# A hybrid mLSTM and GLA layer: alpha by stacked halves, the last norm with features on partitions, and three reorderings

## The reference

```
h = rmsnorm(x, g1) * (1 + scale1) + shift1 ;  z = h @ w_in
la = log_sigmoid(lr_b @ w_alpha + b_alpha) / 16      # rank 16, 4 heads of 128: the forget gates of GLA
x  = x + gate1 * ((sig(g_a) * mlstm(...) + sig(g_b) * gla(q_b, k_b, v_b, la)) @ w_out)
h2 = rmsnorm(x, g2) * (1 + scale2) + shift2
x  = x + gate2 * ((silu(h2 @ w_gate) * (h2 @ w_up)) @ w_down)
y  = rmsnorm(x, g_final)                             # the last norm
```

## Time and profile before

| what | us |
| --- | --- |
| median of 3 runs | 1948.06 (1946.88 to 1949.89) |
| the profiled execution, whole | 1946.07 |
| its span, first to last instruction | 1944.3 |
| TensorE busy in the span | 1897.1 |
| VectorE, ScalarE, GpSimd busy | 1062.3, 681.8, 681.9 |

### The profile page before, as it was taken

One profiled execution on the slowest core, in us unless ns is written; L12 is line 12 of the kernel. 1 busy time (PEld: TensorE's weight loads), 2 busy tenths in 40 slices (PEclk: granted clock), 3 DMA queues, 4 the chain that ended last, 5 costly groups with the idle time before them and its releaser, 6 DMA issues. The chain is left out here.

```text
span 1944.3 us, 33250 instructions
## 1 busy us (share of the span) xinstructions
PE 1897.1 (98%) x13205; PEld 1813.6 (93%) x13205; DVE 1062.3 (55%) x1900; ACT 681.8 (35%) x1425; POOL 681.9 (35%) x582
## 2 busy tenths in 40 slices
PE   7899999999999999999999999999999999999997
PEld 4899999999999989999898999999999999999996
DVE  5740554414553226534164578786756666566657
ACT  4523423334234243342343554322232223322333
POOL 3221322212232213313132485334454345444541
PEclk8999999999999999999999999999999999999999
DMA  9241222332222322224133553102121112111212
GB/s 335 72 100 50 74 77 55 105 84 69 71 62 73 104 79 71 55 62 128 54 85 105 176 157 99 44 23 66 44 66 42 47 45 66 50 39 44 66 44 101
DMA packets 211266, 155.07 MB, mean 80 GB/s; under 512 B 10196, under 2 KB 195732, under 8 KB 210600
## 3 DMA queue, kind: packets, MB, share of 16 engines
q1 hardware_dynamic: 210810, 152.73, 26.6%
q10 hardware_dynamic: 302, 0.22, 0.0%
HBM read 131.42 MB, written 21.50 MB: 79 GB/s over the span
## 5 line engine op out<-in xcount | busy, mean ns | idle before, releaser
L1264 POOL TENSOR_TENSOR w_lo<-w_raw,w_hi 128x512 fp32r<-128x512 f32 x128 | 180.5, 1410 | 714.6 <-ACT w_hi L1087 714.6
L919 PE MATMUL bank<-h_hi,w_hi 128*128 128x352 f32 x1536 | 328.7, 336 | 1.3 <-ACT w_hi L1087 1.3
L919 PE MATMUL bank<-h_hi,w_lo 128*128 128x352 f32 x1536 | 313.4, 326 | 1.2 <-POOL w_lo L1264 1.1
L919 PE MATMUL bank<-h_lo,w_hi 128*128 128x352 f32 x1536 | 312.9, 325 | 0.0
L919 PEld LDWEIGHTS bank<-h_hi,w_hi 128*128 128x128 f32 x1536 | 257.0, 190 | 16.5 <-issue 12.1
L919 PEld LDWEIGHTS bank<-h_hi,w_lo 128*128 128x128 f32 x1536 | 260.3, 190 | 2.7 <-POOL w_lo L1264 2.7
L919 PEld LDWEIGHTS bank<-h_lo,w_hi 128*128 128x128 f32 x1536 | 260.4, 190 | 0.0
L2287 POOL TENSOR_TENSOR f_lo<-w_raw,f_hi 128x512 fp32r<-128x512 f32 x107 | 143.0, 1341 | 201.8 <-ACT f_hi L2111 201.7
L2287 POOL TENSOR_TENSOR w_lo<-w_raw,w_hi 128x512 fp32r<-128x512 f32 x107 | 144.2, 1352 | 149.3 <-ACT w_hi L2111 149.2
L2625 DVE SCALAR_TENSOR_TENSOR x_t<-bank,ada,x_t 128x352 f32<-128x352 f32 (+1 forms) x288 | 156.1, 568 | 56.0 <-PE bank L2042 38.8
L1087 ACT ACTIVATE w_hi<-w_raw 128x512 fp32r<-128x512 f32 x128 | 80.1, 626 | 166.4 <-PE bank L919 166.4
(11 more groups left out here) (480 smaller groups left out, 3864.5 us busy)
## 6 DMA issues: line engine op xcount, KB each, us to landing
w_raw<-in_w_in SPq DMA_DIRECT2D x128, 256.0 KB, 3.0
w_ada_tile<-in_w_ada SPq DMA_DIRECT2D x32, 512.0 KB, 4.3
w_raw<-in_w_out SPq DMA_DIRECT2D x48, 256.0 KB, 2.9
w_raw<-in_w_ffn_gate SPq DMA_DIRECT2D x44, 256.0 KB, 3.0
w_raw<-in_w_ffn_up SPq DMA_DIRECT2D x44, 256.0 KB, 3.0
w_raw<-in_w_ffn_down SPq DMA_DIRECT2D x44, 256.0 KB, 2.7
w_ada_ring<-in_w_ada SPq DMA_DIRECT2D x8, 1024.0 KB, 7.8
x_scratch<-x_turned_rows SPq DMA_DIRECT2D x1, 4224.0 KB, 14.0
```

What stands on the lines that cost most here:

```text
L919: last = pe.matmul(g.ps[b][:, 0:n], x[:, s, k, :], y[:, 4 * h + k, c0:c0 + n], start=(h == 0 and k == 0 and m == 0), stop=(h == 1 and k == ...
L1264: pool.tensor_tensor(Wl[:, s], raw[:, r], Wh[:, s].bitcast(F32), ALU.subtract).then_inc(s_lo, 1)
```

## The change

- Alpha. Three groups of 16 rows are stacked at partitions 0, 32 and 64 of `xal` (high, low, high half of the inputs) and of `wal` (high, high, low half of the weights), in fp32r, with zeros between, so one product sums the three. Four heads times three matmuls of 352 columns replace the float32 ones. New stages `alpha_hi` and `alpha_lo` of head 0 make the halves on ScalarE and VectorE. `rows` and the loaded weights (three loads) live in a buffer of the values `v_b` until that is filled; the small loads and the first evacuation wait for x to be stored.
- `ada3` and `level0` of window A go from slot 39 to 40.
- In the first `out` step of the last third, ScalarE's square of the step before comes ahead of the two `h2_hi`.
- `last_third` replaces the last two pieces of the first plain unit: first weight half of gate and of up, then second half of each.
- In the first seven-product unit ScalarE makes weight halves 3 and 4 ahead of the product copies, and t copies 14 and 15 go between later halves; VectorE takes `form(15)` and the low halves 14 and 15 behind the first addition.
- The last norm with features on partitions. In the last down block ScalarE squares each piece of x and scales it in place by the gain, GpSimd adds the squares of features groups 1 to 6 into 352 columns a third, VectorE adds the last. TensorE multiplies these sums by a column of ones, which gives a mean square per token in a bank; root, reciprocal, and after the transposes VectorE scales the left and ScalarE the right half of each row tile. Six banks instead of eight serve the transposes. The gains, 8 numbers per partition, are loaded in the middle of `out`.

The diff, cut to its core:

```diff
-    "A": [("decay", 1), ("ada_load0", 2), ("scores", 6), ("keys", 6), ("interq", 8),
+    "A": [("decay", 1), ("ada_load0", 2), ("alpha_hi", 3), ("alpha_lo", 9), ("scores", 6), ("keys", 6), ("interq", 8),
...
-        rows = sb("gate_rows", [P, T])
+        setup_rows = V[1][:, :, :].rearrange("p n v -> p (n v)")
+        rows, w_rows = setup_rows[:, 0:T], setup_rows[:, T:T + QK]
+        xal = sb("alpha_inputs", [P, T], F32R)
...
-        wal = sb("w_alpha_all", [P, QK])
+        wal = sb("w_alpha_all", [P, QK], F32R)
...
-                     (m0[:, :], a["state_m"][0].rearrange("b h -> h b")), (wal[64:64 + RANK, :], a["w_alpha"][0])]
+                     (m0[:, :], a["state_m"][0].rearrange("b h -> h b"))]
+            small += [(w_rows[r:r + RANK, :], a["w_alpha"][0]) for r in (0, 32, 64)]
...
+            sp.wait_ge(g.s_xst, 16)
...
-                        for b, (c0, m) in enumerate(PARTS):
-                            full(pe.matmul(use(n + b)[:, 0:m], wal[64:64 + RANK, i * DK:(i + 1) * DK], rows[64:64 + RANK, c0:c0 + m], start=True, stop=True))
+                        pe.wait_ge(s_rows, 4)
+                        for c in range(NPC):
+                            c0, m = span(c)
+                            full(pe.matmul(use(n + c)[:, 0:m], wal[0:64 + RANK, i * DK:(i + 1) * DK], xal[0:64 + RANK, c0:c0 + m],
+                                           start=True, stop=True))
...
+                    elif name == "alpha_hi" and i == 0:
+                        act.wait_ge(s_r3, 1)
+                        for r in (0, 64):
+                            act.activation(xal[r:r + RANK, :], rows[64:64 + RANK, :], ACT.Copy)
+                        for r in (0, 32, 64):
+                            last = act.activation(wal[r:r + RANK, :], w_rows[r:r + RANK, :], ACT.Copy)
+                        last.then_inc(s_rows, 1)
+                    elif name == "alpha_lo" and i == 0:
+                        act.wait_ge(s_rows, 3)
+                        act.activation(xal[32:32 + RANK, :], rows[64:64 + RANK, :], ACT.Copy)
+                        act.activation(wal[64:64 + RANK, :], w_rows[64:64 + RANK, :], ACT.Copy).then_inc(s_rows, 1)
...
+                    elif name == "alpha_hi" and i == 0:
+                        dve.wait_ge(s_rows, 2)
+                        dve.tensor_tensor(rows[64:64 + RANK, :], rows[64:64 + RANK, :], xal[64:64 + RANK, :].bitcast(F32), ALU.subtract)
+                        dve.tensor_tensor(w_rows[64:64 + RANK, :], w_rows[64:64 + RANK, :], wal[64:64 + RANK, :].bitcast(F32),
+                                          ALU.subtract).then_inc(s_rows, 1)
...
+            def last_third(pl):
+
+                c0, n = span(NPC - 1)
+                pe.wait_ge(s_smh, 1)
+                for h in range(2):
+                    pe.wait_ge(s_hh, (NPC - 1) * KC + 4 * h + 4)
+                    for t in range(2):
+                        bnk, turns = pl.piece(3 * t + NPC - 1)
+                        if h == 0:
+                            wait(pe, s_pf[bnk], turns)
+                        s, _, before = pl.half(2 * t + h)
+                        pe.wait_ge(s_hi, before + 1)
+                        for m, (x, y) in enumerate(((Wh, g.Hh), (Wh, g.Hl), (Wl, g.Hh))):
+                            if m == 1 and t == 0:
+                                pe.wait_ge(s_sml, 1)
+                                pe.wait_ge(s_hl, (NPC - 1) * KC + 4 * h + 4)
+                            if m == 2:
+                                pe.wait_ge(s_lo, before + 1)
+                            for kk in range(4):
+                                last = pe.matmul(g.ps[bnk][:, 0:n], x(s)[:, kk, :], y[:, 4 * h + kk, c0:c0 + n],
+                                                 start=(h == 0 and kk == 0 and m == 0), stop=(h == 1 and kk == 3 and m == 2))
+                        if (h, t) != (0, 1):
+                            last.then_inc(s_used, 1 + h * t)
...
+            def mean_squares(c):
+
+                pe.wait_ge(s_fm, c + 1)
+                if c < 2:
+                    bnk, turns = lastp.piece(22 + c)
+                    pe.wait_ge(s_pf[bnk], turns + 1)
+                else:
+                    pe.wait_ge(s_rt, NPC + 1)
+                for t in DONE_WITH[c]:
+                    n = P if t < NC else NS
+                    last = pe.matmul(MS[c][0:n, t:t + 1], SQX[:, t * P:t * P + n], one, start=True, stop=True)
+                last.then_inc(s_sum, 1)
...
+            turn(0)
+            mean_squares(0)
+            turn(1)
+            mean_squares(1)
+            turn(2)
+            mean_squares(2)
+            for t in range(3, NT):
+                turn(t)
...
+                        square(b - 1)
                         h2_hi(c - 2, KC - 2)
                         h2_hi(c - 2, KC - 1)
                     if c and n > 1:
                         h2_hi(c - 1, n - 2)
-                    if b:
+                    if b and (c < 2 or n):
...
+                if nth(f) == 0:
+                    t_hi(12, 13)
                 hi(pl, 3)
                 if nth(f) == 0:
-                    t_hi(12, 13)
+                    hi(pl, 4)
...
-                    t_hi(14, 15)
-                hi(pl, 4)
-                hi(pl, 5)
+                    t_hi(15)
...
+            def last_square(k):
+
+                n, c = divmod(k, NPC)
+                c0, w = span(c)
+                bnk, turns = lastp.piece(k)
+                act.wait_ge(s_pf[bnk], turns + 1)
+                m = k - NPC
+                if m < 0:
+                    act.wait_ge(s_al, acts(FT))
+                    dst = SQX[:, c0:c0 + w]
+                else:
+                    if m >= NSQ:
+                        act.wait_ge(s_sqa, 18 + m - NSQ + 1)
+                    dst = SQR[m % NSQ]
+                act.activation(dst, X[:, n, c0:c0 + w], ACT.Square).then_inc(s_sq, 1)
+
+            def last_gain(k):
+
+                n, c = divmod(k, NPC)
+                c0, w = span(c)
+                act.wait_ge(s_sq, 24 + k + 1)
+                if k == 0:
+                    act.wait_ge(s_gf, 16)
+                act.activation(X[:, n, c0:c0 + w], X[:, n, c0:c0 + w], ACT.Copy, scale=gain[:, n:n + 1]).then_inc(s_fs, 1)
...
+            late = NPC * (KC - 1)
+            for k in range(NPC * KC):
+                if k == late:
+                    last_gain(k - 1)
...
+            for k in range(NPC, NPC * (KC - 1)):
+                c0, w = span(k % NPC)
+                m = k - NPC
+                pool.wait_ge(s_sq, 24 + k + 1)
+                if m >= NPC:
+                    pool.wait_ge(s_sqa, 18 + m - NPC + 1)
+                pool.tensor_tensor(SQX[:, c0:c0 + w], SQX[:, c0:c0 + w], SQR[m % NSQ], ALU.add).then_inc(s_sqa, 1)
...
-                    form(14, 15)
-                    t_lo(14)
-                    t_lo(15)
-                    dve.wait_ge(s_tfl, 16)
+                    form(14)
                 combine_third(f)
+                if nth(f) == 0:
+                    dve.wait_ge(s_tfl, 14)
                 for q in range(2):
                     wait_product(dve, pl, P6, q)
                     made(P1, q)
                     dve.tensor_tensor(U1[q], P1C[q], bank(P6, q), ALU.add).then_inc(freed(P6, q), 1)
+                if nth(f) == 0:
+                    form(15)
+                    t_lo(14)
+                    t_lo(15)
+                    dve.wait_ge(s_tfl, 16)
...
+            def last_sum(c):
+
+                c0, w = span(c)
+                k = NPC * (KC - 1) + c
+                dve.wait_ge(s_sq, 24 + k + 1)
+                dve.wait_ge(s_sqa, 18 + k - NPC - NPC + 1)
+                dve.tensor_tensor(SQX[:, c0:c0 + w], SQX[:, c0:c0 + w], SQR[(k - NPC) % NSQ], ALU.add).then_inc(s_fm, 1)
+
+            def inverse_of(c):
+
+                t0, t1 = DONE_WITH[c][0], DONE_WITH[c][-1] + 1
+                dve.wait_ge(s_rt, NPC + c + 1)
+                dve.reciprocal(RI[:, t0:t1], RT[:, t0:t1]).then_inc(s_fr, 1)
...
+                dve.tensor_scalar(OT[0:n, t % NXR, 0:512], ENDB[2 * (t % NE)][0:n, :], RI[0:n, t:t + 1], None, ALU.mult).then_inc(s_fo, 1)
...
+            for c in range(NPC):
+                last_sum(c)
+            for c in range(NPC):
+                inverse_of(c)
+                if c < 2:
+                    left_half(c)
+            for t in range(2, NT):
+                left_half(t)
```

More of the change, by code:

```diff
@@ L1194, in window @@
                     elif name == "alpha":
-                        for b, (c0, m) in enumerate(PARTS):
-                            wait_use(act, w, i, n + b)
-                            last = act.activation(QD[:, c0:c0 + m], RB(n + b)[:, 0:m], ACT.Copy)
-                            last.then_inc(free(n + b), 1)
+                        for c in range(NPC):
+                            c0, m = span(c)
+                            wait_use(act, w, i, n + c)
+                            last = act.activation(QD[:, c0:c0 + m], RB(n + c)[:, 0:m], ACT.Copy)
```

(56 more changed lines are left out.)

67 lines of the change are left out of this document (33 added, 34 removed), and 2 rows, old and new, of the table AT_SLOT.

## The result

The changed kernel takes **1927.59 us** (median of four runs, 1924.94 to 1928.20) against 1947.47 (1946.82 to 1949.89) for the kernel before: a ratio of 0.9899, with a 95% interval of 0.9887 to 0.9910, so 19.7 us less (17.5 to 22.0). The forecast was 1927.3. The sum behind it fits less well than that figure does, and the terms have to be read one by one. The profiled execution took 1924.94, with a span of 1923.1.

The account below looks back on a forecast made before the run. TensorE, busy 98% of the span, was taken to bound the kernel. Savings 6.3 + 4.5 + 1.0 + 1.5 + 1.2 - 0.2 + 6.5 = 20.8 off the profiled 1946.07, plus 1.99 to the median, gave 1927.3 us; range 1919.5 to 1936.

Parts of the forecast that it names:

- Alpha's products: Forget-gate products per head: three single-pass matmuls take 0.49 us instead of 2.06, saving 6.3 us over four heads.
- The clock behind alpha: After alpha of heads 1 to 3 the low clock no longer comes: 4.5 us saved, bounds 0 and 4.8.
- The rival's reason: Low clock stays after alpha because it fell only 1 to 2 us after alpha's start; 1931.8 us, chance 0.14.
- Level 0: At head 0, one piece later, TensorE no longer waits 0.99 us for its input: 1.0 us saved.
- The square: Norm sum in the output projection: square moved ahead of two h2 copies removes TensorE's wait, 1.5 us saved, bounds 0.5 and 1.5.
- The last third: Weight halves reordered: a wait of 0.6 to 0.9 us replaces 1.81 at the eighth h2 feature, 1.2 us saved.
- The first seven-product tile: Stop of 2.74 us goes, TensorE waits some 3 us in the down block: -0.2 us saved, bounds -1.5 and +3.
- part 4: The reordering of weight halves and t copies in the first seven-product tile, forecast to save -0.2 us.
- The tail: After the last addition: earlier first store 2.8, closer stores 3.3, sample rows 0.4; 6.5 us saved, bounds 2 and 9.
- ScalarE's backlog: Last down block: squares and gains cost 0.8 us a piece against TensorE's 0.96, so eight early pieces' backlog clears by the end.
- The spacing: Output stores in the tail leave 1.3 us apart instead of 1.77, bounds 1.05 and 1.6.
- The rival "slower": Last block: GpSimd's additions stretch VectorE's to 1417 to 1620 ns a piece, ending at 1950 or 1957 us; chance 0.03.

Follow-up runs that it names:

- part 5 alone: Only the last norm's hunks of the diff put into the kernel before: 1942.03 us against 1947.06, ratio 0.9972.
- Part 1 alone: Only alpha's hunks (stages `alpha_hi` and `alpha_lo`, stacked halves, slot 40) put into the kernel before: 1934.23 us against 1947.06, ratio 0.9935.

## Why the prediction was right, step by step

**Alpha's products: right**, 5.84 for 6.3. A group costs 0.59, not 0.49.

**The clock behind alpha: the effect right** (4.86 for 4.5), the cause half seen. I named the length; in the runs length and few rows stand together. The rival's reason was misread: the fall at 461.04 comes 2.4 us after alpha's start and 0.3 after its end, not 1 to 2 us after the start.

**Level 0: right**, 1.15 for 1.0; one piece later, no wait.

**The square: half right.** "TensorE wants it at 1168.2" held, and 1.82 was saved on the spot. The step that failed is the silent one, that a lead gained there is kept: VectorE needs 8.76 us where TensorE needs 7.8, and 1.05 went back. Net 0.77 for 1.5, inside the bounds.

**The last third: right**, 1.07 for 1.2, with the new wait where it was named.

**The first seven-product tile: right.** +0.9 less 0.75 times 1.5 was the forecast. VectorE's last step of the activations ends 27.9 us after the tile's start, where it was 28.9, so 0.9 earlier. The stops in the down block are 2.3 us for "some 3". Without the fall of the clock it is +0.97, with it -0.56 to -0.63. The fall came in five of nine kernels, so part 4 pays nothing in the mean.

**What no term held:** 0.52 on the way to the first seven-product tile, where TensorE, which now comes earlier, waits 0.26 us in the first down block for GpSimd's low half of the activations; that break and the restart behind it are the 0.52.

**The tail: the sum right** (5.85 in this profile, 6.6 in the one with part 5 alone, for 6.5), its parts less so. GpSimd was done at 1905.93, 0.5 before the last addition's end, not two us behind it: an addition took 0.91, for 1.0, and the first started 16.9 us before that end, for 16. That ScalarE's backlog "is gone by the end" was wrong: a square and a gain take 0.87 together, and 1.0 at the very end, for 0.8; they run without a gap and set the first root. The first store came 3.0 us behind the last addition, where 4.2 was forecast. The spacing, 1.27 for 1.3, is luck: seven runs have 1.09 to 1.15. But the transfers then trail by 1.16 us more at the end (3.51 for 2.35), and in all first store to end takes 13.6, or 12.8 to 13.0 in those seven, where the sum had 12.5 (16.2 less 3.3 and 0.4).

**The rival "slower" was summed wrongly**, which touches no other number: at 1.62 us a piece 24 additions end 24 times 0.66, 15.8 us, late, not 23; the 23 holds the sample rows' eight times 0.9 already, so its two times are 1943 and 1950, not 1950 and 1957. Its reason did not come true: the additions of x kept 0.57.

**The agreement to 0.3 us is partly luck.** The two profiles differ by 21.1 us. Of that 1.71 is set-up, for which the prediction had no gain, and 1.36 the last window; without them 18.1 is left of a forecast 20.8. The set-up's 1.71 is no more than it varies by: with the changed set-up code it took from 60.3 to 63.3 us in twelve profiles. Part 1 alone and part 5 alone measure 12.8 and 5.0. The measured difference of the medians, 19.7, has an interval of 17.5 to 22.0, and holds both.

## What to carry to other kernels

A stop that is removed pays only as far as the next engine in the chain can follow: compare that engine's time per step with TensorE's over the next tens of us before the gain is booked. Where several small products with few rows in use are summed, stack them along the rows: here that saved 1.04 us a head, 4.2 in all. The other 1.7 of alpha's own gain came with the number format, and the 4.9 of the clock came without stacking too, in nine products that took 1.63 us. And where a reordering moves a stop from a covered place to an uncovered one, count the low clock that may follow it.

## What the hardware showed that was not expected

- The granted clock went with the rows in use: thirteen products of 352 columns with 16 rows were followed by 0.50 at three of four heads, thirteen with 80 rows by 1.00 at all four (one execution each; where alpha meets the clock was not held fixed).
- Whether the clock falls at a doubtful place differs between executions with the same code up to there. Seven of the kernels run here have the changed kernel's mixer code, itself among them: five needed 1021.5 to 1021.6 us for it and two 1024.5, with the clock down in the last window. The Trainium skill (TensorE: Matmul & The Clock Gate, Part 1) says that the chip's watch on TensorE runs free of the kernel, so that one kernel meets it at different phases; these runs agree. A single profile can thus carry 3 us of it either way.
- VectorE's additions from a bank kept their time beside GpSimd's (567 ns in the mean over 288, 568 before), but the last small one with two SBUF inputs went from 0.19 to 0.93 us in the last block, and back to 0.19 without GpSimd's additions. That is the rule of the Trainium skill that the prediction weighed (SBUF — State Buffer, Who interferes with whom), at a place where I had priced it only in the slower rival; here ScalarE's row hid the cost.
